# A hybrid decoder step on one core: a sample's compressed cache pieces added up by accumulating gathers, and gated products kept in their PSUM bank

## The reference, cut to what matters

```
proj = einsum('blnc,ncd->blnd', branches, w_branch)
gate = sigmoid(einsum('bld,de->ble', h, w_gate) + b_gate)
x = x + einsum('bld,de->ble', sum(gate * proj over branches), w_out)
```

```
s16 = kv_cmp.reshape(B, n16, CMP_STRIDE, 2, KVH_D, HD_D).sum(axis=2)
cmp = (s16[:, :-1] + s16[:, 1:]) / CMP_BLOCK
```

## Time and profile before

| | before |
|---|---|
| median of 3 runs | 1323.42 us (1317.82 to 1324.16) |
| profiled execution | 1319.65 us |
| its span, first to last instruction | 1317.8 us |
| PE busy | 1223.6 us, 93% |
| DVE busy | 557.1 us, 42% |
| POOL busy | 505.1 us, 38% |
| ACT busy | 438.1 us, 33% |
| mean granted TensorE clock | 0.968 of full speed |

### The profile page before, as it was taken

The page is one execution under the profiler, slowest core; times in us unless marked ns, Lnnn a source line. Parts: engine busy times, 40 slices in busy tenths (PEclk is TensorE's granted clock), DMA queues, the critical chain, the costliest instruction groups (busy, mean ns, idle before and its releaser), DMA issues.

```text
span 1317.8 us, 24302 instructions
## 1 busy us (share of the span) xinstructions
PE 1223.6 (93%) x10336; PEld 1147.7 (87%) x10336; DVE 557.1 (42%) x895; ACT 438.1 (33%) x708; POOL 505.1 (38%) x262
## 2 busy tenths in 40 slices
PE   6999989988998888889998978999999999999998
PEld 6998879977988877778887756899999999999998
DVE  4156644451427666664666555553322100222002
ACT  5242321123453223344544233243443211334110
POOL 3274431353134564322222353444344343443440
PEclk8999999988999999899999899999999999999999
DMA  4320111641035463411113385322222222222222
GB/s 183 145 81 33 35 63 57 151 113 65 33 114 193 156 199 129 156 49 65 49 49 129 92 311 206 129 92 86 97 89 87 96 82 93 96 80 95 89 88 81
DMA packets 47160, 139.52 MB, mean 106 GB/s; under 512 B 4454, under 2 KB 16074, under 8 KB 46682
## 3 DMA queue, kind: packets, MB, share of 16 engines
q1 hardware_dynamic: 36706, 100.50, 22.9%
q0 software_dynamic: 10368, 37.75, 8.4%
HBM read 129.98 MB, written 8.49 MB: 105 GB/s over the span
## 4 chain that ended last, share of the span: by engine, by line
PE 78%; DVE 12%; DMA 4%; ACT 2%; issue 2%; POOL 2%; SPq 1%; DVEq 0%; ACTq 0%
PE PS L607 44%; PE PS L837 11%; PE PS L652 7%; PE PS L706 2%; PE PS L972 2%; DMA M<-cache_cmp_kv,idx 2%; DVE M L1775 1%; PE PS L1001 1%; DMA M<-cache_slc_kv,idx 1%; PE PS L985 1%; PE PS L1030 1%; DVE M L1778 1%; DVE xT L1642 1%; PE PS L800 1%; DMA M<-weights 1%
## 5 line engine op out<-in xcount | busy, mean ns | idle before, releaser
L2175 POOL TENSOR_TENSOR WL<-M,WH 128x1024 fp32r<-128x1024 f32 x159 | 389.7, 2454 | 709.1 <-ACT WH L1179 708.8
L1179 ACT CAST WH<-M 128x1024 fp32r<-128x1024 f32 x159 | 165.7, 1046 | 281.4 <-DMA M<-weights 281.4
L607 PE MATMUL PS<-hH,WH 128*128 128x260 f32 x1040 | 214.2, 287 | 11.1 <-DVE M L1610 5.8
L607 PE MATMUL PS<-hH,WL 128*128 128x260 f32 x1040 | 211.5, 285 | 0.0
L607 PE MATMUL PS<-hL,WH 128*128 128x260 f32 x1040 | 211.5, 285 | 0.0
L607 PEld LDWEIGHTS PS<-hH,WH 128*128 128x128 f32 x1040 | 163.1, 192 | 14.7 <-issue 9.8
L607 PEld LDWEIGHTS PS<-hH,WL 128*128 128x128 f32 x1040 | 162.5, 191 | 0.0
L607 PEld LDWEIGHTS PS<-hL,WH 128*128 128x128 f32 x1040 | 162.4, 191 | 0.0
L837 PE MATMUL PS<-hH,WH 128*128 128x260 f32 x384 | 115.6, 301 | 5.3 <-ACT tmp L1332 3.2
L837 PE MATMUL PS<-hL,WH 128*128 128x260 f32 x384 | 111.7, 291 | 0.0
L837 PE MATMUL PS<-hH,WL 128*128 128x260 f32 x384 | 111.5, 290 | 0.0
(11 more groups left out here) (382 smaller groups left out, 2240.4 us busy)
## 6 DMA issues: line engine op xcount, KB each, us to landing
M<-weights SPq DMA_DIRECT2D x159, 512.0 KB, 3.3
M<-cache_win_kv POOLq DMA_DIRECT2D x7, 512.0 KB, 5.4
spill<-xT SPq DMA_DIRECT2D x1, 2080.0 KB, 8.3
M<-spill SPq DMA_DIRECT2D x1, 2080.0 KB, 7.7
M<-x_prompt SPq DMA_DIRECT2D x4, 512.0 KB, 5.5
y_prompt<-M SPq DMA_DIRECT2D x4, 512.0 KB
con<-tables SPq DMA_DIRECT2D x1, 1437.5 KB, 12.3
M<-state_gla SPq DMA_DIRECT2D x2, 512.0 KB, 6.6
```

What stands on the lines that cost most here:

```text
L607: last = mm(PS[:, bank + h, 0:HALF], w[:, slot_of(n), k, :], x[:, HALF * h:HALF * h + HALF], start=(start and k == k0 and w is WH and x is ...
L1179: nc.scalar.copy(WH[:, at].rearrange("p k n -> p (k n)"), WR[:, at]).then_inc(sem("w_hi"), 1)
L2175: p.tensor_tensor(WL[:, at].rearrange("p k n -> p (k n)"), WR[:, at], WH[:, at].rearrange("p k n -> p (k n)"), ALU.subtract).then_inc(sem( ...
```

## The change

Two things are changed.

First, a sample's four pieces are gathered into one slot. The first gather writes, and the other three are accumulating gathers, in which the DMA adds the gathered rows to what the slot holds. Each has to wait for the one before it on the same slot, and this wait stands on POOL. Three samples are in turn, one in each slot of the ring; a table says behind which step POOL issues which piece (`C_GATHER`), behind which DVE folds a sample (`C_FOLD`), behind which PE multiplies (`C_PRODUCT`), and behind which DVE copies out (`C_COPY`). DVE does two additions for a sample (1024 to 512 wide, 512 to 256 wide).

Second, the gated product for k of 32 and more, and that of the last branch, is written back to its own PSUM bank, and the addition to `mixT` reads it there. The scratch tile `GP` and the wait for its readers go. The bank counts as free when the addition is done (`mix_add`).

```
 def mix_evac(k):
-    return ("sg" if gate else "mix_mul"), 16 * bi + 4 * m + 2 * t + h + 1
+    u = 16 * bi + 4 * m + 2 * t + h + 1
+    return ("sg", u) if gate else ("mix_add", u - 16) if bi else ("mix_mul", u)
...
+        C_GATHER = {k: (n, c) for a, b, at in ((0, 3, -1), (3, 6, 15), (6, 8, 30)) for c in range(4)
+                    for n in range(a, b) for k in [at + 3 * c + n - a]}
+        C_FOLD = {12: 0, 13: 1, 14: 2, 28: 3, 29: 4, 30: 5, 42: 6, 43: 7}
+        C_PRODUCT = {15: (0, 1), 18: (2,), 31: (3,), 34: (4, 5), 45: (6, 7)}
+        C_COPY = {16: 0, 32: 2, 35: 4, 46: 6}
+        CSUM = [zt[:, 4, T:T + 512], zk[:, 1536:2048], zk[:, 512:1024]]
...
-                    if bi > 1 or bi and u > 18:
-                        dve.wait_ge(sem("mix_add"), u - 16 - 2)
-                    out = GP[:, half] if bi else mixT[:, 2 * m + t, half]
+                    bank = PS[:, mix_bank(k), 0:HALF]
+                    out = bank if bi else mixT[:, 2 * m + t, half]
...
-                        v.tensor_tensor(mixT[:, 2 * m + t, half], mixT[:, 2 * m + t, half], GP[:, half], ALU.add)\
+                        v.tensor_tensor(mixT[:, 2 * m + t, half], mixT[:, 2 * m + t, half], bank, ALU.add)\
...
+                if k in C_FOLD:
+                    n = C_FOLD[k]
+                    w, total = CRING[n % 3], CSUM[n % 3]
+                    dve.wait_ge(sem(f"xc{n % 3}"), 64 * (n // 3 + 1))
+                    if n >= 3:
+                        dve.wait_ge(sem("c_mm"), n - 2)
+                    v.tensor_tensor(total, w[:, 0:512], w[:, 512:1024], ALU.add).then_inc(sem("c_free"), 1)
+                    dve.wait_ge(sem("c_free"), n + 1)
+                    v.tensor_tensor(total[:, 0:256], total[:, 0:256], total[:, 256:512], ALU.add)\
+                        .then_inc(sem("c_fold"), 1)
...
+            def compressed_gather(n, c):
+
+                if n >= 3 and c == 0:
+                    gp.wait_ge(sem("c_free"), n - 2)
+                if c:
+                    gp.wait_ge(sem(f"xc{n % 3}"), 16 * (4 * (n // 3) + c))
+                at = NI + NS * c + CSAMPLES[n]
+                src, row = rows("cache_cmp_kv"), bass.IndirectOffsetOnAxis(idx[:, at:at + 1], 0)
+                if c:
+                    gp.indirect_dma_start(CRING[n % 3], None, src, row, compute_op=ALU.add).then_inc(sem(f"xc{n % 3}"), 16)
```

More of the change, by code:

```diff
@@ L473, in last_evac @@
             kind = LAST[e][0]
-            return sem("sg" if kind == "g" else "mix_mul"), 48 + sum(x[0] == kind for x in LAST[:e + 1])
+            count = sum(x[0] == kind for x in LAST[:e + 1])
+            return (sem("sg"), 48 + count) if kind == "g" else (sem("mix_add"), 32 + count)
         block = ctx.enter_context(nc.Block())
@@ L839, in mix_step @@
                 last.then_inc(sem("prod"), 1)
-                if k % 6 == 2 and 8 <= k <= 50:
-                    compressed_sum((k - 8) // 6)
+                for c in C_PRODUCT.get(k, ()):
+                    compressed_sum(c)
             def compressed_sum(n):
@@ L848, in compressed_sum @@
                     pe.wait_ge(sem("sh_ev"), n // 2)
[L849 removed]
+                mm(PS[0:NCMP, 5, 256 * (x % 2):256 * (x % 2) + 256], C("shift", 0, NCMP), CSUM[n % 3][:, 0:256],
                    start=True, stop=True).then_inc(sem("c_mm"), 1)
@@ L1115, in _ @@
                 if n == 3:
-                    pe.wait_ge(sem("mix_mul"), 56)
+                    pe.wait_ge(sem("mix_add"), 40)
                 if n >= 3:
@@ L1757, in mix_step @@
                     dve.wait_ge(sem("sg"), u)
-                    if bi > 1 or bi and u > 18:
-                        dve.wait_ge(sem("mix_add"), u - 16 - 2)
-                    out = GP[:, half] if bi else mixT[:, 2 * m + t, half]
-                    v.scalar_tensor_tensor(out, SG[t][:, half], 1.0, PS[:, mix_bank(k), 0:HALF], ALU.add, ALU.mult)\
+                    bank = PS[:, mix_bank(k), 0:HALF]
+                    out = bank if bi else mixT[:, 2 * m + t, half]
+                    v.scalar_tensor_tensor(out, SG[t][:, half], 1.0, bank, ALU.add, ALU.mult)\
                         .then_inc(sem("mix_mul"), 1)
@@ L1764, in mix_step @@
                         dve.wait_ge(sem("mix_mul"), u)
-                        v.tensor_tensor(mixT[:, 2 * m + t, half], mixT[:, 2 * m + t, half], GP[:, half], ALU.add)\
+                        v.tensor_tensor(mixT[:, 2 * m + t, half], mixT[:, 2 * m + t, half], bank, ALU.add)\
                             .then_inc(sem("mix_add"), 1)
[L1767 to L1783, removed]
+                if k in C_FOLD:
[8 more added lines that the diff above has]
+                        .then_inc(sem("c_fold"), 1)
+                if k in C_COPY:
+                    n = C_COPY[k]
                     x = CSAMPLES[n]
@@ L2116, in _ @@
                 dve.wait_ge(sem("prod"), units_before(N_LAST) + e + 1)
-                dve.wait_ge(sem("mix_add"), 32 + k)
-                v.scalar_tensor_tensor(halves(GP), halves(SG4[2 * (m % 2) + t]), 1.0, pair(LAST_PAIR[e]), ALU.add, ALU.mult)\
+                banks = pair(LAST_PAIR[e])
+                v.scalar_tensor_tensor(banks, halves(SG4[2 * (m % 2) + t]), 1.0, banks, ALU.add, ALU.mult)\
                     .then_inc(sem("mix_mul"), 1)
                 dve.wait_ge(sem("mix_mul"), 48 + k + 1)
-                v.tensor_tensor(mixT[:, k], mixT[:, k], GP, ALU.add).then_inc(sem("mix_add"), 1)
+                v.tensor_tensor(halves(mixT[:, k]), halves(mixT[:, k]), banks, ALU.add).then_inc(sem("mix_add"), 1)
                 if k:
@@ L2239, in _ @@
             rows = lambda name: A[name].rearrange("o n (r t) a k d -> (o n r) (t a k d)", t=4)
[L2241 to L2248, removed]
+            def compressed_gather(n, c):
[7 more added lines that the diff above has]
+                    gp.indirect_dma_start(CRING[n % 3], None, src, row, compute_op=ALU.add).then_inc(sem(f"xc{n % 3}"), 16)
+                else:
+                    gp.indirect_dma_start(CRING[n % 3], None, src, row).then_inc(sem(f"xc{n % 3}"), 16)
             def mix_step(k):
@@ L2255, in mix_step @@
                     lower(N_MIX + 12 * bi + 3 * m + 1 + (s + 1) // 2)
[L2256 to L2259, removed]
+                if k >= 2 and k in C_GATHER:
+                    compressed_gather(*C_GATHER[k])
             def cache_piece(n):
@@ L2265, in cache_piece @@
                 if n == 0:
-                    gp.wait_ge(sem("c_free"), len(CPIECES))
+                    gp.wait_ge(sem("c_free"), NS)
                 if n == 2:
@@ L2287, in _ @@
             gp.wait_ge(sem("prod"), units_to_free(N_MIX - 4))
-            compressed_gather(0)
-            compressed_gather(1)
-            compressed_gather(2)
+            for n in range(3):
+                compressed_gather(n, 0)
             lower(N_MIX)
```

3 lines of the change are left out of this document (removed).

## The result

The changed kernel runs in 1308.12 us (median of 9 runs, 1297.90 to 1315.44) against 1323.42 us. Over all runs of the two kernels the ratio is 0.9877, with a 95% interval of 0.9851 to 0.9903: 1.2% faster. (It is not exactly the quotient of the two medians, 0.9884.) The profiled execution took 1308.94 us, 10.7 us less than that of before.

The account below looks back on a forecast made before the run. PE's 25.1 us of idleness, mostly behind DVE's piece additions, and a lowered clock (up to 9.9 us) were taken to bound steps 0 to 47. −21 − 5 − 2 + 2 + 3.8 = −22.2 us gives 1297.5, median 1300; range 1288 to 1316.

Parts of the forecast that it names:

- the rival of another wait: Steps 0 to 47: attention or weight chain replaces half of PE's old waits; whole gain about 9 us, 1312; chance 0.22.
- DVE's work: Compressed pieces in steps 0 to 47: additions and folds take 8.9 to some 12 us in place of 55.9.
- Waits, −21: Steps 0 to 47: PE's 22.7 us of waits behind DVE's piece additions nearly go; 21 us taken back.
- Last gather of the second turn, +2: Behind step 30: DVE, and PE with it, stalls for sample 5's last piece; costs 2 us, bounds 0 to 4.
- The new wait on POOL: Steps 0 to 47: POOL waits one or two us for landings ahead of lower parts; PE loses nothing.
- The DMA engines' load: Accumulating gathers may double transfer time, adding 37 us of engine time; DMA share 0.74 at most, weights still ahead of need.
- The clock, −5: Steps 0 to 47: slow stretches behind PE's idle times mostly go; 5 us back, bounds 0 and 7.3.
- The adding line: Additions to `mixT` reading the bank cost 0.43 us each in place of a mean 0.744; 2 us gained.
- The held bank, +3.8: Product steps 36 to 63: bank freed 0.46 us later, by the addition; costs 3.8 us, bounds 0 and 7.
- both bank terms: Products in their bank: 2 us gained from unstretched additions, 3.8 us lost by the later release of the bank.
- Slow gathers (0.10): First two turns: landings of L us starve PE by 2 × 3 × (L − 8.5); 1335 us at L = 15; chance 0.10.

Follow-up runs that it names:

- both moves: Changed kernel with gathers issued earlier and the second turn's folds two steps later: 1291.3 us, ratio 0.9750 to the kernel before.

## Why the prediction came out as it did

The direction and the range were right (1288 to 1316, measured 1308.12), the size was not: 22.2 us were forecast from the profiled time, 10.7 came, and 15.3 by the medians. The measured time lies just above the forecast's own range (1289 to 1308), in that of the rival of another wait; the wider range holds because it took in both. The old waits went as forecast; that new ones took their place, through late landings, was not in the forecast.

- **DVE's work**: right in count, a little low in size. 15.5 us in place of 55.9; I had said 9 to 12. The difference is stretches of L1777 and L1779 (means of 1.456 and 0.678 us where 0.69 and 0.42 are undisturbed).
- **Waits, −21**: this is the term that was mis-sized. The old mechanism was right: the transposes' 8.6 us are down to 0.7, and the split's 4.0 are gone. But PE's waits in steps 0 to 47 still sum to 15.7 us, 11.3 of them of a new kind: 7.1 behind folds whose gathers landed late (2.8 of these by the stretch of the fold behind step 28) and 4.2 behind lower parts. Of the 25.1 us of idleness, 25.1 − 15.7 = 9.4 came back, where I had put 21.
- **Last gather of the second turn, +2**: the step that failed. I placed the wait behind step 30 and at the last sample only. It stands at the first sample of both turns, behind steps 12 and 28 (3.79 and 3.38 us), and cost 7 us in steps 0 to 47 in place of 2, as the run with late folds shows (10.1 us back in steps 0 to 31, 3.2 lost again in 32 to 47); earlier gathers with the folds unmoved gave 8.3 us back in steps 0 to 31. I had reckoned one landing behind the last issue. The last piece of sample 5 was issued when I had said, 89.6 us behind the start of step 0 (89.7 by my sum). What I did not reckon with is the first sample of a turn: its last piece comes at the end of a chain of landings in its slot, for each of which POOL waits, and those that set the pace took 9.5 to 10.5 us in place of the 7 us that I took.
- **The new wait on POOL, "at nothing for PE"**: wrong by 4.2 us. POOL waited 14.1 us for landings, and three lower parts came late. Earlier gathers halved POOL's waits and left 3.0 us of PE's.
- **The DMA engines' load**: right. 24 × 1.54 = 37 us of engine time were put down for the second read; the software queue took 141 us (10.8% of 1307) in place of 111, 30 us more. The share was 0.78 in steps 0 to 31 and 0.70 in steps 0 to 47 together, under my bound of 0.74 for that stretch. Plain gathers and late folds, one without this load and one with it, differ by 0.8 us in steps 0 to 31. By the rule of the Trainium skill that I named (Collectives: The Full Stack, "The bandwidth ceiling: the fold count and why AG ≠ RS ≠ AR") the estimate is 37 us; the measured 30 us are near it. That the second read is what makes them is not shown, as the profile counts the same bytes. For the landing my estimate by the same rule of the Trainium skill, some 1.5 us more for a piece, was too low: at the same places the 24 gathers took 8.8 us (median) where plain ones took 5.6.
- **The clock, −5**: 2.4 us came back in steps 0 to 47 (3 + 4.4 us lost before, 5.0 after). The slow stretches went where their waits went, and new ones came behind new waits; with both moves the clock is full in steps 0 to 47.
- **The adding line**: right. Its mean fell from 0.744 to 0.425 us:

```profile
L1769 DVE TENSOR_TENSOR xT<-xT,PS x32: 424/425/425, 517.4 to 733.0; 128x260 f32<-128x260 f32 x32
```

- **The held bank, +3.8**: the gap behind product steps 36 to 47 is 0.98 us in place of 0.52, as forecast. It costs PE 2.1 us in six waits. The net of both bank terms was put at +1.8 us; by the medians it measured −3.7 alone and +0.8, −4.4 and −1.1 in company, so its sign was not borne out.
- **The rivals**: a new wait in the place of the old one (0.22) is what half happened, with the weight chain (POOL's lower parts) that it names beside the attention chain, but set off by the gathers; the attention's waits went. Slow gathers (0.10) has the other half of the mechanism: with the measured median of 8.8 us its formula gives 2 × 3 × 0.3 = 1.8 us where PE waited 4.2 for lower parts, and it does not have the waits on DVE at all. In all these the landing was put too low.

## What to carry to other kernels

A DMA that adds into its own slot makes a chain: count the landings in a row, each from its issue to its landing, before fixing where the result is used. Three landings here took 30 us, one behind the other, where plain gathers into slots of their own need not wait for each other. If such a consumer waits in order ahead of work that others need, move it by a step or two first, or start the chain earlier; here either gave 6 to 7 us in steps 0 to 47 and both 11 us, on top of the 9.6 us that the whole change had given there, and cost no instruction. And where one engine's queue is relieved, look at who now stands in an order table with a wait: POOL got 14 us of them.

## What the runs showed of the hardware that I had not expected

- An accumulating gather of 128 rows of 4 KB keeps POOL for 1.55 us against 0.94 to 0.96 for a plain one, and its median landing is 8.8 us against 5.6 for a plain one at the same places.
- The first 50 us, which no edit touches, ran at a granted clock of 0.83 in the profile of the changed kernel and of 0.93 in that of before, and step 0 began 6.4 us later.
- Waits of PE of only 1.8 to 2 us were followed by slow stretches of 5 us at 0.64 to 0.66 of the clock (steps 12 and 28 of the changed kernel), so a short wait can cost as much again. It need not: with both moves a wait of 1.80 us at 474.55 was followed by full speed, so part of what that kernel gained in steps 0 to 31 may be luck.

```profile
474.50:479.50 5.00, 4.95 (x41) 4.95 (x42) 1.19 (x3) 1.05 (x1) 2.40 (x1) 1.00 1.05 252
```
